# A two-layer hybrid decoder trunk: the mixer's steps in a new order, and sums over feature blocks added by VectorE ahead of one multiplication by ones

## The chip, the cores and the metric

The kernel runs on one NeuronCore of one Trainium2 chip. The metric is the device time of one execution in microseconds (us). The times before the change are 2061.08, 2059.67 and 2060.58 us, median 2060.58. A difference under 0.2%, about 4.1 us, can't be told from none.

## The reference

The input is x (1, 256, 1024), with 256 memory tokens of the same width, all float32. There are two layers (0 and 1), each of three parts with a residual sum behind each:

```
h = h + mixer(rms_norm(h, g_mix))          # 9 column groups of one input projection, three branches, w_out
h = h + cross_attention(rms_norm(h, g_x), rms_norm(mem, g_mem))
h = h + ffn(rms_norm(h, g_f))              # layer 0: dense SwiGLU; layer 1: top 2 of 8 experts
out = rms_norm(h, g_final)
```

The mixer's branches are: A, `silu(layer_norm(conv31(c_a * sigmoid(c_b)))) @ w_conv_out`, where conv31 is a causal depthwise convolution of 31 taps over 512 channels; B, a pooling mixer with a small product `pool_w` and `@ w_pool_out`; C, an mLSTM of 4 heads whose hidden state is normed per head, gated by `sigmoid(z)` and multiplied by `w_mlstm_out`. Each branch is scaled by a sigmoid gate (ga, gb, gc, 1024 columns each), the three are added and multiplied by `w_out`. An RMS norm needs the sum of h² over 1024 features, the layer norm the sum of u and of (u - mean)² over 512.

## The kernel before

**Layout and staging.** Activations lie features first: a tile `[128, 8, 256]` has feature k·128+p in partition p of block k, and 256 tokens. So a sum over features is a sum over partitions and over blocks. TensorE makes it by multiplying with an all-ones matrix, one 256-column product for each block, added in PSUM. All weights pass in chunks of 1 MB (`[128, 2048]` float32): SP loads a chunk into one of 3 `raw` tiles; ScalarE writes its rounded part to one of 3 `w_hi` tiles (`split` on `act`, L685); VectorE writes the rest to `w_lo` (`split` on `dve`, L1079 through `lo`); TensorE makes three products for each block (L1656 to L1658, hi·hi, hi·lo, lo·hi). A chunk of the mixer is 48 products of 256 columns. A `w_hi` tile is free when TensorE has finished the chunk three before it (`pe_chunk`), and SP loads the chunk three on when the VectorE half is done.

**Order.** `MIX` names the mixer's 63 chunks in TensorE's order: cb, ca, q, k, v, pu, z (input columns); gb0, gb1, pw, gb2, gb3; wp0, wp1 (pool output, two PSUM banks each); gc0 to gc3; wm0 to wm3 (mLSTM output); ga0 to ga3; wc0, wc1 (conv output); wo0 to wo3 (w_out); xk0 to xk3, xv0, xq0 to xq3, xv1 to xv3, xo0 to xo3 (attention). Layer 0 then has 33 dense chunks (ff), layer 1 the experts. The programs of ScalarE and VectorE walk the same list by hand: for a step c they do `post(c - 3)`, all work on what chunk c - 3 gave, and then `split(c)`. All engines take their instructions in the order written.

**Places that the change touches.**
- `conv31` deals the taps out to steps by `TAPS`, behind the split; `merge` (wp, wm) multiplies a product in PSUM by its gate and adds it to `xf`. `merge_conv` (wc0, wc1) does that in two halves each and, for each half, waits for ScalarE's rounded part (`merged_hi`, L772) and writes the rest to `a_lo` (`merged_lo`).
- `HIDDEN_T` is the step of gc0. Behind that chunk TensorE turns the normed hidden state (`hidden_transpose`, L1789), for which ScalarE must have scaled it (L840) by reciprocals that VectorE makes (L1310) in step 27. `HIDDEN_STD` is step 26.
- Layer norm: `ln_sums` (L1795) behind wm1 for the sum, behind wm3 for the squares, 4 products each.
- `project_two`: wo0 and wo1 go together. First come blocks 0 to 3 of both, then blocks 4 to 7 of both, so that `a_lo` may be late for the second half.
- `sum_squares` (L1721) is 2 products for each quarter of h. ScalarE squares a quarter into one of two halves of `sq` (in `cacc`). The norm ahead of attention (n = 1) has its quarters behind wo2, wo3, xk0 and xk1; `std` and the norm itself are in ScalarE's and VectorE's step xk1. The norm ahead of the dense part (n = 2, layer 0) has them behind xo1, xo2, xo3 and ff0. Layer 1 has `router_pair` in its place: for each quarter, 4 products for the router's logits (L1731) and 4 for the squares (L1739), tokens in the rows.

Of the kernel before, what the change touches and what calls it, by code (L numbers as in the profile page):

```python
# [22 lines left out]
ALU = mybir.AluOpType  # L23
# [3 lines left out]
P = 128  # L27
# [27 lines left out]
MIX += [("gb", 0), ("gb", 1), ("pw", 0), ("gb", 2), ("gb", 3)] + [("wp", i) for i in range(2)]  # L55
MIX += [("gc", i) for i in range(4)] + [("wm", i) for i in range(4)]
# [128 lines left out]
def trunk(nc, w, out):  # L185
    ctx = ExitStack()
    with ctx:
# [129 lines left out]
        tok_rst, m_scaled = sem("token_rstd"), sem("mem_scaled")  # L317
# [3 lines left out]
        squared = sig("squared", 12)  # L321
        summed = sig("squares_summed", 12)
# [19 lines left out]
        c31_done = sig("conv_done", 1)  # L342
# [334 lines left out]
        def _(act):  # L677
# [116 lines left out]
            def post(layer, j):  # L794

# [17 lines left out]
                elif j in GATE_NO:  # L813
                    gate(layer, j)
                elif kind == "xk":
                    multiplied(layer, j)
                    act.activation(flat(k_t[:, 2 * i:2 * i + 2, :]), bank(("chunk", j))[:, :], ACT.Copy).then_inc(xk_done.sem, 1)

                if j == GATE_ROWS:
                    forget_rows(layer)  # L820
# [41 lines left out]
                if kind == "wc":  # L862
                    for q in (2 * i, 2 * i + 1):
                        merged_hi(layer, q)
# [9 lines left out]
                if XQ0 + 1 <= j < XQ0 + 1 + HEADS:  # L874
                    x_exp(layer, j - XQ0 - 1)
                if XQ0 + 2 <= j < XQ0 + 2 + HEADS:
                    x_copy(layer, j - XQ0 - 2)
                for hd in X_OUT_AFTER.get(j, ()):
                    x_out_hi(layer, hd)
                if XO0 <= j < N_MIX:  # L880
                    if layer and j == XO0:
                        act.activation(warm, eps[:, 0:1], ACT.Sqrt)
                    act.wait_ge(h_att.sem, h_att.at(layer, j - XO0 + 1))
                    if layer == 0:
                        for n in (2 * (j - XO0), 2 * (j - XO0) + 1):
                            ins = act.activation(b_hi[:, n, :], h[:, n, :], ACT.Copy, scale=col(0, R_NORM + 16 + n))
                        ins.then_inc(n_hi.sem, 1)
                    square(layer, 2, j - XO0)
                    if layer:
                        for k in (2 * (j - XO0), 2 * (j - XO0) + 1):  # L890
                            ins = act.activation(xf[:, k, :], h[:, k, :], ACT.Copy, scale=col(0, R_NORM + 16 + k))
                        ins.then_inc(xg_done, 1)
# [35 lines left out]
            def mem_scale():  # L928
                act.wait_ge(tok_rst, 1)
# [8 lines left out]
            def mixer(layer):  # L938
# [6 lines left out]
                if layer:  # L945
                    split(layer, SPL)
                    std(layer, 0)
                    post(layer, 0)
# [92 lines left out]
            for i in range(4):  # L1041

                act.wait_ge(tok_t, 4 + i + 1)
                if i == 0:
                    act.wait_ge(tok_rst, 2)
# [28 lines left out]
        def _(dve):  # L1074
# [63 lines left out]
            def conv31(layer, j):  # L1138

                for pair, k in TAPS.get(j, ()):  # L1140
                    dve.wait_ge(u_done.sem, u_done.at(layer, pair + 1))
                    for c in (2 * pair, 2 * pair + 1):
# [4 lines left out]
                        else:  # L1147
                            ins = dve.tensor_scalar(dst, src, tap, col(0, R_CB + c), ALU.mult, ALU.add)
                        if k == CONV_K - 1 and c == CB - 1:
                            ins.then_inc(c31_done.sem, 1)  # L1150
                        else:
# [1004 lines left out]
```

## Time and profile before

| | before |
|---|---|
| median of three runs | 2060.58 us |
| the profiled execution's own time | 2059.43 us |
| its span, first to last instruction | 2057.7 us |
| TensorE (PE) busy | 2025.9 us, 98% |
| VectorE (DVE) busy | 1631.0 us, 79% |
| ScalarE (ACT) busy | 1304.1 us, 63% |
| mean granted TensorE clock | 0.996 |

In profile lines, PE is TensorE (PEld its weight loads), DVE VectorE, ACT ScalarE and SP the engine that issues the DMAs. A number behind | is busy time, the next the mean of one instruction in ns. Idle time before a group stands with what ended it. A busy PE is counted to the modelled ends of its products, which overlap: the time that a product costs in a stream is the distance of two starts. A float32 product is two records of the profile. In the span, layer 0's mixer and attention last to about 427 us, the dense part to 611, layer 1's mixer and attention to 1036, and the experts to the end.

### The profile page before, as it was taken

The page shows a single profiled execution, that of the slowest core. Times are in us where ns is not written, and L with a number is a line of the kernel's source. Part 1 is how long each engine was busy: PE and PEld are TensorE (multiplying, and loading weights), DVE is VectorE, ACT ScalarE, POOL GpSimd, SP SyncE. Part 2 cuts the span into 40 slices and gives each one's busy share as a digit, 9 for nine tenths or more (in the row PEclk, how much of TensorE's full clock was granted, in tenths as well). Part 3 has the DMA queues.
Part 4 walks back from the last instruction along what each step waited for, and adds up shares of the span by engine and source line. Part 5 has one row for each costly group of instructions (what it writes and reads, how often), then busy time and mean ns, then how long its engine had stood idle before and what let it go on. Part 6 is the DMA issues. An engine that isn't in the chain of part 4 may idle for free.

```text
span 2057.7 us, 33552 instructions
## 1 busy us (share of the span) xinstructions
PE 2025.9 (98%) x12937; PEld 1843.8 (90%) x12937; DVE 1631.0 (79%) x1652; ACT 1304.1 (63%) x1168; POOL 9.3 (0%) x65
## 2 busy tenths in 40 slices
PE   8999999999999999999999999999999999999997
PEld 8999999999999999999988888888888888888886
DVE  6988866555558988866578898888889888898887
ACT  6666454444346566554467777777777777777776
POOL 0000000000000000000000000000000000000000
PEclk9999999999999999999999999999999999999999
DMA  8545545455554545555469999898999989999995
GB/s 251 174 129 165 185 161 187 138 161 189 184 184 142 183 132 164 170 190 164 161 242 375 335 368 372 321 381 325 367 363 345 375 325 370 342 365 375 321 379 188
DMA packets 309916, 527.23 MB, mean 256 GB/s; under 512 B 13598, under 2 KB 156598, under 8 KB 309814
## 3 DMA queue, kind: packets, MB, share of 16 engines
q1 hardware_dynamic: 309814, 525.81, 73.0%
q8 instruction: 72, 1.18, 0.2%
q14 instruction: 30, 0.25, 0.0%
HBM read 524.73 MB, written 1.05 MB: 256 GB/s over the span
## 4 chain that ended last, share of the span: by engine, by line
PE 80%; DVE 9%; ACT 5%; issue 4%; SPq 1%; DMA 0%; DVEq 0%; ACTq 0%
PE ps L1656 25%; PE ps L1658 24%; PE ps L1657 24%; DVE w_lo L1079 3%; ACT w_hi L685 2%; DVE c L1146 1%; PE ps L2027 1%; ACT w_hi L692 1%; PE ps L2102 1%; PE ps L1806 1%; PE ps L1826 1%; DVE a_lo L1079 1%; PE ps L1721 1%; DVE xf L1103 0%; PE ps L1770 0%
## 5 line engine op out<-in xcount | busy, mean ns | idle before, releaser
L1079 DVE TENSOR_TENSOR w_lo<-raw,w_hi 128x2048 fp32r<-128x2048 f32 (+1 forms) x330 | 752.5, 2282 | 246.9 <-ACT w_hi L685 181.9
L1656 PE MATMUL ps<-w_hi,a_hi 128*128 128x512 f32 (+1 forms) x1472 | 566.2, 385 | 2.2 <-DVE w_lo L1079 2.2
L1658 PE MATMUL ps<-w_hi,a_lo 128*128 128x512 f32 (+1 forms) x1472 | 560.5, 381 | 0.0
L1657 PE MATMUL ps<-w_lo,a_hi 128*128 128x512 f32 (+1 forms) x1472 | 559.6, 380 | 0.0
L1656 PE MATMUL ps<-a_hi,w_hi 128*128 128x256 f32 x1456 | 417.4, 287 | 4.0 <-DVE xf L1197 1.9
L1657 PE MATMUL ps<-a_lo,w_hi 128*128 128x256 f32 x1456 | 412.0, 283 | 0.0
L1658 PE MATMUL ps<-a_hi,w_lo 128*128 128x256 f32 x1456 | 411.8, 283 | 0.0
L692 ACT ACTIVATE w_hi<-raw 128x2048 fp32r<-128x2048 f32 x171 | 328.1, 1919 | 122.4 <-PE ps L1658 122.4
L685 ACT ACTIVATE w_hi<-raw 128x2048 fp32r<-128x2048 f32 (+1 forms) x159 | 299.9, 1891 | 59.0 <-PE ps L1658 42.7
L1658 PEld LDWEIGHTS ps<-w_hi,a_lo 128*128 128x128 f32 x1472 | 276.6, 188 | 53.6
L1656 PEld LDWEIGHTS ps<-w_hi,a_hi 128*128 128x128 f32 x1472 | 276.9, 188 | 53.0 <-DVE w_lo L1079 2.8
L1657 PEld LDWEIGHTS ps<-w_lo,a_hi 128*128 128x128 f32 x1472 | 277.0, 188 | 50.7
L1656 PEld LDWEIGHTS ps<-a_hi,w_hi 128*128 128x128 f32 x1456 | 279.2, 192 | 5.7 <-issue 2.2
L1657 PEld LDWEIGHTS ps<-a_lo,w_hi 128*128 128x128 f32 x1456 | 279.3, 192 | 0.5
L1658 PEld LDWEIGHTS ps<-a_hi,w_lo 128*128 128x128 f32 x1456 | 279.1, 192 | 0.0
L1656 PE MATMUL ps<-b_hi,w_hi 128*128 128x256 f32 x808 | 231.5, 286 | 2.5 <-DVE w_lo L1079 1.4
L1657 PE MATMUL ps<-b_lo,w_hi 128*128 128x256 f32 x808 | 228.6, 283 | 0.0
L1658 PE MATMUL ps<-b_hi,w_lo 128*128 128x256 f32 x808 | 228.6, 283 | 0.0
L1656 PEld LDWEIGHTS ps<-b_hi,w_hi 128*128 128x128 f32 x808 | 155.0, 192 | 4.0 <-DVE w_lo L1079 1.8
L1657 PEld LDWEIGHTS ps<-b_lo,w_hi 128*128 128x128 f32 x808 | 155.0, 192 | 0.3
L1658 PEld LDWEIGHTS ps<-b_hi,w_lo 128*128 128x128 f32 x808 | 155.0, 192 | 0.0
L1079 DVE TENSOR_TENSOR w_lo<-mem_t,w_hi 128x2048 fp32r<-128x2048 f32 x56 | 128.4, 2292 | 21.6 <-ACT w_hi L692 21.6
(314 smaller groups left out, 2144.6 us busy)
## 6 DMA issues: line engine op xcount, KB each, us to landing
raw<-in_moe_w SPq DMA_DIRECT2D x171, 1024.0 KB, 6.0
raw<-in_w_in SPq DMA_DIRECT2D x68, 1024.0 KB, 5.2
mem_t<-in_moe_w SPq DMA_DIRECT2D x56, 1024.0 KB, 5.7
area<-in_moe_w SPq DMA_DIRECT2D x56, 1024.0 KB, 5.7
xf<-in_moe_w SPq DMA_DIRECT2D x56, 1024.0 KB, 5.3
raw<-in_ffn_w SPq DMA_DIRECT2D x33, 1024.0 KB, 5.3
raw<-in_w_mlstm_out SPq DMA_DIRECT2D x8, 1024.0 KB, 5.0
raw<-in_w_out SPq DMA_DIRECT2D x8, 1024.0 KB, 5.0
```

The source lines that it names most:

```text
L685: act.activation(w_hi[c % SPL][:, 0:n], raw[c % RAW][:, 0:n], ACT.Copy).then_inc(hi_done.sem, 1)
L692: act.activation(w_hi[m % SPL][:, :], e_raw[m % ERAW][:, 0:CH], ACT.Copy).then_inc(e_hi.sem, 1)
L1079: return dve.tensor_tensor(dst, whole, as_f32(hi), ALU.subtract)
L1146: ins = dve.scalar_tensor_tensor(dst, src, tap, dst, ALU.mult, ALU.add)
L1656: pe.matmul(dst, wh, xh, start=start, stop=False, skip_group_check=True)
L1657: pe.matmul(dst, wh, xl, start=False, stop=False, skip_group_check=True)
L1658: return pe.matmul(dst, wl, xh, start=False, stop=stop, skip_group_check=True)
L1721: ins = pe.matmul(ps[4][:, 0:T], ones[:, :], sq[:, j % 2, i * T:(i + 1) * T], start=(j == 0 and i == 0), stop=(j == 3 and i == 1), skip_gr ...
L1806: ins = pe.matmul(ps[4 + hd % 2][:, tt * T:(tt + 1) * T], q_t[:, k, tt * P:(tt + 1) * P], k_t[:, k, :], start=(tt == 0 and e == 0), stop=( ...
L1826: ins = pe.matmul(ps[X_OUT_BANK[hd]][:, e * T:(e + 1) * T], vx[:, m, hd, e * P:(e + 1) * P], z_sig[:, 4 + 2 * (hd % 2) + m, :], start=(e = ...
L2027: ins = pe.transpose(ps[6][:, k * P:(k + 1) * P], act_e[g % 2][:, k * P:(k + 1) * P], ident[:, :])
L2102: ins = pe.matmul(ps[7 - i][:, k * P:(k + 1) * P], h_tok[:, tt, c:c + P], sel[:, tt, :], start=(k == 0 and tt == 0), stop=(tt == 1), skip_ ...
```

## The change

1. In `MIX`, gc0 moves ahead of wp1. With it `HIDDEN_T` becomes step 28 instead of 29.
2. `post` is cut in two. For a step c, both engines do `first(c - 3)`, `split(c)`, `later(c - 3)`. `first` has what frees PSUM banks, with the merges, `merge_conv` with `merged_hi`, the residual sums and the attention steps. `later` has what remains.
3. `project_two` becomes `project_three`: wo0, wo1 and wo2 go together in the two halves.
4. For three norms (n = 1 of both layers, n = 2 of layer 0) VectorE adds the quarters of squares into one block (`add_squares`), and TensorE makes one product with ones (`sum_added`) instead of eight. It stands behind xk1 for n = 1, and behind ff0 for n = 2. From the third quarter on, ScalarE's square waits for the sum of the quarter before.
5. The layer norm's terms are added by VectorE over blocks (`add_blocks`), one product each instead of four. 
6. In layer 1, three of the router norm's quarters are added by VectorE; the products for squares are 8 at the end instead of 16 spread over the four quarters.
7. One semaphore less: `tok_rst` is replaced by higher counts of `x_scaled`.

```diff
-MIX += [("gb", 0), ("gb", 1), ("pw", 0), ("gb", 2), ("gb", 3)] + [("wp", i) for i in range(2)]
-MIX += [("gc", i) for i in range(4)] + [("wm", i) for i in range(4)]
+MIX += [("gb", 0), ("gb", 1), ("pw", 0), ("gb", 2), ("gb", 3), ("wp", 0), ("gc", 0), ("wp", 1)]
+MIX += [("gc", i) for i in range(1, 4)] + [("wm", i) for i in range(4)]
...
             def square(layer, n, j, src=h):
-                act.wait_ge(summed.sem, summed.at(layer, 4 * n + j - 1))
-                act.activation(sq[:, j % 2, :], flat(src[:, 2 * j:2 * j + 2, :]), ACT.Square).then_inc(squared.sem, 1)
+                if n == 0:
+                    act.wait_ge(summed.sem, summed.at(layer, j - 1))
+                elif j == 0:
+                    act.wait_ge(summed.sem, summed.at(layer, 4 * n))
+                elif j > 1:
+                    act.wait_ge(sq_add.sem, sq_add.at(layer, 3 * (n - 1) + j - 1))
+                act.activation(sq[:, j % 2 if n == 0 else min(j, 1), :], flat(src[:, 2 * j:2 * j + 2, :]), ACT.Square).then_inc(squared.sem, 1)
...
+            def add_squares(layer, n, j):
+
+                dve.wait_ge(squared.sem, squared.at(layer, 4 * n + j + 1))
+                if j > 1:
+                    dve.wait_ge(sq_add.sem, sq_add.at(layer, 3 * (n - 1) + j - 1))
+                ins = dve.tensor_tensor(sq[:, 0, :], sq[:, 0, :], sq[:, 1, :], ALU.add)
+                if j == 3:
+                    ch.link(ins)
+                    ins = dve.tensor_tensor(sq[:, 0, 0:T], sq[:, 0, 0:T], sq[:, 0, T:2 * T], ALU.add)
+                ins.then_inc(sq_add.sem, 1)
+
+            def add_blocks(src, done):
+
+                ch.link(dve.tensor_tensor(cacc[:, 0:2, :], src[:, 0:2, :], src[:, 2:4, :], ALU.add))
+                dve.tensor_tensor(cacc[:, 0, :], cacc[:, 0, :], cacc[:, 1, :], ALU.add).then_inc(done.sem, 1)
...
+                if j == LN_MEAN + 1:
+                    dve.wait_ge(ln_sq.sem, ln_sq.at(layer, 1))
+                    add_blocks(cacc, ln_added)
...
+                if WO0 + 2 <= j < WO0 + 5:
+                    add_squares(layer, 1, j - WO0 - 1)
+                if XO0 + 2 <= j < N_MIX:
+                    add_squares(layer, 2, j - XO0 - 1)
...
                 for c in range(SPL + layer, N_MIX + SPL):
-                    post(layer, c - SPL)
+                    first(layer, c - SPL)
                     if c < N_MIX:
                         split(layer, c, chunk_len(c))
+                    later(layer, c - SPL)
...
-            def project_two(layer, c, xh, xl, ready):
+            def project_three(layer, c, xh, xl, ready):
 
                 for part in range(2):
-                    for j in (c, c + 1):
+                    for j in (c, c + 1, c + 2):
                         if part == 0:
                             pe.wait_ge(lo_done.sem, lo_done.at(layer, j + 1))
                             take_banks(layer, ("chunk", j))
...
+            def sum_added(layer, n):
+                pe.wait_ge(sq_add.sem, sq_add.at(layer, 3 * n))
+                pe.matmul(ps[4][:, 0:T], ones[:, :], sq[:, 0, 0:T], start=True, stop=True).then_inc(summed.sem, 1)
+                pe.sem_inc(summed.sem, 3)
...
+            def router_squares(layer):
+
+                pe.wait_ge(sq_add.sem, sq_add.at(layer, 5))
+                for s in range(2):
+                    if s:
+                        pe.wait_ge(squared.sem, squared.at(layer, 12))
+                    for i in range(2):
+                        for tt in range(TT):
...
+            def ln_sums(layer, done):
+                pe.matmul(ps[5][:, 0:T], ones[:, :], cacc[:, 0, :], start=True, stop=True).then_inc(done.sem, 1)
...
                     if c == LN_MEAN:
-                        pe.wait_ge(c31_done.sem, c31_done.at(layer, 1))
-                        ln_sums(layer, c31, ln_sum)
+                        pe.wait_ge(ln_added.sem, ln_added.at(layer, 1))
+                        ln_sums(layer, ln_sum)
                     if c == LN_VAR:
-                        pe.wait_ge(ln_sq.sem, ln_sq.at(layer, 1))
-                        ln_sums(layer, cacc, ln_var)
+                        pe.wait_ge(ln_added.sem, ln_added.at(layer, 2))
+                        ln_sums(layer, ln_var)
...
-                    if WO0 + 2 <= c < WO0 + 6:
-                        sum_squares(layer, 1, c - WO0 - 2)
+                    if c == WO0 + 5:
+                        sum_added(layer, 1)
...
                     if j == 0:
-                        sum_squares(layer, 2, 3)
+                        sum_added(layer, 2)
```

## Rows read from the trace of the kernel before

**Rows 1.** The page: busy us, share and instructions; granted TensorE clock in 40 slices.

```profile
PE 2025.9 (98%) x12937; PEld 1843.8 (90%) x12937; DVE 1631.0 (79%) x1652; ACT 1304.1 (63%) x1168; POOL 9.3 (0%) x65
...
PEclk9999999999999999999999999999999999999999
```

**Rows 2.** Waits of PE: us in total, how many, longest us.

```profile
PE ps L1656 <- DVE w_lo L1079: 6.3, 9, 1.3
...
PE ps L1656 <- DVE xf L1197: 1.9, 2, 0.9
PE ps L1656 <- DVE a_lo L1079: 1.8, 2, 0.9
...
PE ps L1656 <- issue: 1.1, 2, 0.5
```

**Rows 3.** PE's timeline, layer 0: start us, us, what, [idle before, its releaser].

```profile
192.09 0.28 PE L1658 MATMUL ps<-b_hi,w_lo 128*128 128x256 f32 x1
...
294.17 0.28 PE L1658 MATMUL ps<-a_hi,w_lo 128*128 128x256 f32 x1
295.35 0.39 PE L1656 MATMUL ps<-a_hi,w_hi 128*128 128x256 f32 x1 [0.91 <-DVE a_lo L1079]
...
305.41 0.28 PE L1658 MATMUL ps<-a_hi,w_lo 128*128 128x256 f32 x1
...
306.51 0.28 PE L1657 MATMUL ps<-a_lo,w_hi 128*128 128x256 f32 x1
```

**Rows 4.** PE's groups by line and form: count, busy us, mean ns, idle before.

```profile
L1721 PE MATMUL ps<-cacc,ones 128*128 128x256 f32 x64 | 16.1, 378 | 0.0
...
L1739 PE MATMUL ps<-ones,cacc 128*128 128x1 f32 x32 | 4.1, 250 | 0.0
...
L1795 PE MATMUL ps<-cacc,ones 128*128 128x256 f32 x16 | 3.8, 378 | 0.0
```

**Rows 5.** Two stretches: us, busy PE, PEld, DVE, ACT, POOL, PEclk, DMA, GB/s.

```profile
173.87:198.93 25.06, 24.45 (x196) 23.74 (x194) 22.02 (x39) 12.83 (x16) 0.00 (x0) 1.00 0.55 170
263.95:287.08 23.13, 23.13 (x192) 23.13 (x193) 13.14 (x10) 11.46 (x13) 0.00 (x0) 1.00 0.69 227
```

**Rows 6.** DVE's timeline at wc0 to wo3, layer 0.

```profile
280.71 0.68 DVE L1210 TENSOR_TENSOR area<-area,ps 128x512 f32<-128x512 f32 x1
...
296.41 2.29 DVE L1079 TENSOR_TENSOR w_lo<-raw,w_hi 128x2048 fp32r<-128x2048 f32 x1 [1.11 <-ACT w_hi L685]
...
299.21 3.25 DVE L1348 SCALAR_TENSOR_TENSOR b_lo<-mem_t,par,b_hi 128x256 fp32r<-128x256 f32 x8
```

**Rows 7.** ACT's timeline in the same stretch.

```profile
294.48 1.89 ACT L685 ACTIVATE w_hi<-raw 128x2048 fp32r<-128x2048 f32 x1
296.28 3.30 ACT L867 ACTIVATE b_hi<-mem_t,par 128x256 fp32r<-128x256 f32 x8
299.48 0.62 ACT L696 ACTIVATE cacc<-h 128x512 f32<-128x512 f32 x1
```

**Rows 8.** Timeline of the hidden state's scaling and turning, layer 0, all engines.

```profile
198.93 0.20 DVE L1310 RECIPROCAL small<-small 128x8 f32<-128x8 f32 x1
199.04 1.24 DVE L1197 TENSOR_TENSOR xf<-area,ps 128x512 f32<-128x512 f32 x2
199.16 3.31 ACT L840 ACTIVATE q_t<-q_t,small 128x256 f32<-128x256 f32 x8 [4.06 <-DVE small L1310]
...
205.64 1.91 PE L1789 MATMUL ps<-ident,q_t 128*128 128x128 f32 x16
207.30 0.36 PE L1656 MATMUL ps<-a_hi,w_hi 128*128 128x256 f32 x1
```

**Rows 9.** Layer 1's router: DVE's last residual sum; the chain's piece behind it.

```profile
1032.50 0.69 DVE L1217 TENSOR_TENSOR h<-h,ps 128x512 f32<-128x512 f32 x1 [0.64 <-PE ps L1658]
...
1035.94 3.46 PE ps L1998 x16
```

**Rows 10.** The stretch at L1998, as rows 5: the number behind POOL's is PEclk.

```profile
1035.80:1039.20 3.40, 3.40 (x18) 3.40 (x18) 3.03 (x23) 3.20 (x6) 0.00 (x0) 0.50 0.00 0
```

More of the change, by code:

```diff
@@ L1291, in post, with later @@
                     ins.then_inc(u_done.sem, 1)
+                if j == PW:
+                    multiplied(layer, j)
+                    for g in range(NG):
+                        ins = dve.tensor_scalar(pooled[:, g, :], bank(("chunk", j), g // 2)[:, (g % 2) * HALF:(g % 2 + 1) * HALF], col(0, R_PS + g), None, ALU.mult)
+                    ins.then_inc(pw_done.sem, 1)
+                if kind == "wp":
+                    merge(layer, j, 2 * i, 2)
+                if kind == "wm":
+                    merge(layer, j, 4 + i, 1)
+                if kind == "wc":
+                    merge_conv(layer, j, i)
+                if WO0 <= j < XK0:
+                    residual(layer, j, j - WO0, h_mix)
+                if kind == "xv":
+                    x_value(layer, j, i)
+                if kind == "xq":
+                    multiplied(layer, j)
+                    dve.tensor_copy(flat(q_t[:, 2 * i:2 * i + 2, :]), bank(("chunk", j))[:, :]).then_inc(xq_done.sem, 1)
+                if XQ0 + 1 <= j < XQ0 + 1 + HEADS:
+                    x_probs(layer, j - XQ0 - 1)
+                for hd in X_OUT_AFTER.get(j, ()):
+                    x_out(layer, hd)
+                if XO0 <= j < N_MIX:
+                    residual(layer, j, j - XO0, h_att)
+                    if layer == 0 and j > XO0:
+                        gained_lo(j - XO0 - 1)
+            def later(layer, j):
+                kind, i = MIX[j]
+                if j == GATE_ROWS:
+                    dve.wait_ge(if_mul.sem, if_mul.at(layer, 1))
+                    dve.wait_ge(ifb_in.sem, ifb_in.at(layer, 32))
+                    ch.did(dve.tensor_scalar(rows[:, 0, :], ps[5][0:HEADS, 0:T], if_bias[0:HEADS, :], None, ALU.add))
+                    dve.tensor_scalar(rows[:, 1, :], ps[5][32:32 + HEADS, 0:T], if_bias[32:32 + HEADS, :], None, ALU.add).then_inc(if_dve.sem, 1)
+                if j in QK_NO:
+                    conv4(layer, QK_NO[j])
+                if j == GATE_ROWS + 1:
+                    gate_scans(layer)
+                if j == GATE_ROWS + 6:
+                    dve.wait_ge(if_tr.sem, if_tr.at(layer, 1))
+                    dve.tensor_copy(gcols[:, :], ps[6][:, 0:16]).then_inc(gcols_done.sem, 1)
                 if j == AT["pu", 1]:
@@ L1439, in mixer @@
                     gained_lo(3)
+                    add_squares(layer, 2, 3)
                     ahead(layer, SPL - 1)
@@ L1861, in chunk @@
                     if i == 0:
-                        project_two(layer, c, a_hi, a_lo, y_lo)
-                    elif i > 1:
+                        project_three(layer, c, a_hi, a_lo, y_lo)
+                    elif i > 2:
                         project(layer, c, a_hi, a_lo)
@@ L1896, in mixer @@
                     for j in range(2):
-                        sum_squares(layer, 0, j)
+                        sum_squares(layer, j)
                 for c in range(N_MIX):
@@ L1901, in mixer @@
                         for j in range(2, 4):
-                            sum_squares(layer, 0, j)
+                            sum_squares(layer, j)
                     if layer == 0 and c == 0:
```

153 lines of the change are left out of this document (58 added, 95 removed).

## The prediction

> **What bounds the kernel now.** I read the page first. PE is busy 98% of the span at full clock in nearly all of it [rows 1], so what lengthens or shortens PE's stream moves the end one to one, and an edit on DVE or ACT counts only where PE comes to wait for it. Next the waits of PE: 9 for the low part of weights (6.3 us), 2 for a merge (1.9), 2 for `a_lo` (1.8) and 2 put down to "issue" (1.1) [rows 2]. Then PE's timeline: an idle of 0.91 is 295.35 - 294.17 = 1.18 from start to start, less 0.12 for the product itself, so each wait costs about 0.16 more than its idle [rows 3]. In a stretch without waits 192 products take 23.13 us, 0.12 us each, and a chunk of 48 takes 5.76 [rows 5]. Last, DVE's and ACT's timelines, to see what each wait is behind. All sums below are worked on the profiled execution (own time 2059.43, span 2057.7; the 1.7 around it stay). The median is 1.15 above it, and I add that at the end.
>
> **Products removed.** Two float32 products of `sum_squares` stand between 305.41 and 306.51: 1.10 less two ordinary distances of 0.12 is 0.86, so 0.43 each [rows 3], not the 378 ns times two records that the group shows. The 64 records of L1721 are 32 products [rows 4]. Three norms go from 8 to 1: 21 x 0.43 = 9.0 us. L1795 has 16 records for the squares and as many for the sums, 16 products that become 4: 12 x 0.43 = 5.2. L1739 has 16 products of one column in 32 records [rows 4]; 8 go. Their cost lies between 0.12 (an ordinary one) and 0.43; I take 0.22, since their records of 250 ns are shorter by a third but their starts are set by two weight loads: 1.8 us. Together -16.0.
>
> **Waits removed.** With `split` ahead of the taps, `conv4`, hidden-state work and the norm, all nine waits for low parts should go: 6.3 + 9 x 0.16 = 7.7. That includes the one at xv0, behind the attention norm, 1.3 in each layer. The wait for wp0's merge goes as wp1 now stands between: 2.2. The "issue" waits are at wp1, whose low part came late: gc0 takes its place and is ready: 1.4. The wait for `a_lo` in wo1 goes into another (below): 2.1. Together -13.4. The bounds are 0 and this; they are all in reach, as each is only some 1 us late and at least one piece of DVE work over 1.2 us moves behind its split.
>
> **Wait added 1: the weights of wo2.** `first` holds `merge_conv` and `merged_hi`, so the split of wo2 keeps its place behind wc1's merge. Here DVE and ACT hand each quarter to and fro from 280.71 on; ACT's split of wo2 starts at 294.48 and DVE's ends at 296.41 + 2.29 = 298.70 [rows 6, 7]. wo0 begins at 287.08, the end of the second stretch [rows 5]. In `project_three` the first halves of wo0 and wo1 take 5.76, and at 292.84 PE asks for wo2. It waits 5.86 us, where it now waits 1.06. Nothing ahead shortens this: the chain starts from ga3's end, as PE's two chunks wc0 and wc1 do. Two layers: +11.7. Bounds: 0 if the split came first, which the diff doesn't do, and 11.7.
>
> **Wait added 2: hidden state turned a chunk earlier.** wp0's last product starts at 192.09 [rows 3], so gc0 would end at 192.2 + 5.76 = 197.9. L1310 is now at 198.93, and L840 scales until 202.5 [rows 8]. In `later(27)` the reciprocals have wp0's merge (1.24) and a split (2.29) in front. DVE was idle 25.06 - 22.02 = 3.0 us in the stretch before [rows 5], idle that came from splits waiting for ACT and that the new order fills. So I leave L1310 at 198.9 (bounds 198.9 and 202.4). The last scaling then ends at about 202.3 and its turning, a quarter of the 1.7 us from 205.64 to 207.30 [rows 8], at 202.7; unhindered it would be 199.6. +3.1 a layer, +6.2.
>
> **Wait added 3: one product behind xk1.** Its operand is the last `add_squares`, in step xk0 behind the split of xk3. Counted from W, the end of wo2's split: wo0 ends at W + 5.8, wo1 8.6, wo2 11.5, wo3 17.3, xk0 23.0, xk1 28.8. ACT splits wo3 to 7.7, then rounds the memory (3.30) to 11.0; DVE's part of wo3 ends at 10.0 and of the memory (3.25) at 13.2; then residual sum 0.68, split of xk0 2.29, residual sum, split of xk1: 19.1. From here DVE and ACT alternate: add 0.7 (as L1210), square 0.62, ACT's split 1.9, DVE's 2.29, add, square, copy of xk0 0.6, ACT's split 1.9, DVE's 2.29, and two adds 1.1 (the second half as wide, between 0.35 and 0.7) [rows 6, 7]. With a few hundredths for each hand-over and 0.08 saved where two on one engine overlap, it ends at W + 31.4: wait 2.6, two layers +5.2. Bounds: 0.3 without the backlog (a copy, two splits and two adds take 6.0 against a chunk's 5.76) and 3.0.
>
> **Wait added 4: the squares of the layer norm.** Behind wm1 (at M) the sum comes at M + 0.43, DVE is in wm3's split to about M + 1.7 (my estimate, from its backlog with the last taps). Then come a merge, twice 0.7 (as L1210), a split 2.3 and the centring 1.9 (five instructions of 256 columns, each a little under the 0.41 of L1348's eight): M + 7.2. ACT squares 1024 columns (1.1, between the 0.62 for 512 and the 1.9 for 2048) and splits 1.9, DVE splits 2.3 and adds 1.15: M + 13.5 with the hand-overs [rows 6, 7]. wm3 ends at M + 12.0: 1.5 a layer, +3.0 (bounds 0 and 2). The first sum has 2 us to spare.
>
> **Wait added 5: quarters behind xo.** Without sums between, PE is 0.86 a chunk faster there, while DVE and ACT alternate as in wait 3. In layer 0, `gained_lo(2)` comes 0.7 late for the third pair of blocks in ff0: +0.7. In layer 1 DVE now waits 0.64 for the last xo product [rows 9]; after it, xo3 ends 1.8 earlier (two groups of squares moved back) and DVE comes 2.2 behind it, then residual sum 0.7, logits 0.9 and eight products 1.8, so the turning L1998 starts 5.6 behind xo3, not 3.5: +2.1, of which I've counted none yet. Together +2.9. Later work (`std`, the attention norm 4 us later) has a chunk or more to spare before xq0.
>
> **Sum without the clock.** -16.0 - 13.4 + 11.7 + 6.2 + 5.2 + 3.0 + 2.9 = -0.4 us.
>
> **The clock.** PE now never idles over 1.3 us in the mixers. Where it did little, in the router, the granted clock fell to 0.50 (1.2 GHz) at 1035.80 [rows 10] and is back at 2.4 GHz in the page's slices behind [rows 1]; 16 turnings took 3.46 there against 1.7 at full clock [rows 8, 9], 1.7 us lost. A 5.9 us idle is far more than anything there. I take one such stretch behind each wo2 wait, part of it inside the wait: 1.4 each, +2.8; bounds 0 and 3.4.
> The Trainium skill ("TensorE: Matmul & The Clock Gate", Part 1) says the throttled state is the default and that steady activity releases it. By that rule the long waits cost more than their length, and the trace agrees at the router; no row before shows a long idle inside the mixer.
>
> **Forecast.** -0.4 + 2.8 = +2.4: 2061.8 for the profiled execution, about 2063.0 as median.
>
> **Rivals.**
> 1. The clock holds, only the waits are there: 2060.58 - 0.4 = 2060.2. For it: the mixer's activity on both sides is dense. Against: the router's rows.
> 2. Slower: the clock falls behind the waits of 2 to 3 us also (the turning of the hidden state with single products between pauses, the product behind xk1, two layers): 4 x 1.4 = +5.6 more, 2068.6. It passes +0.2% from the second such fall on.
> 3. Faster: wo2's part is there in time, because `merge_conv` doesn't delay the split as read: +11.7 becomes 0 and so does the clock's 2.8: 2060.58 - 12.1 = 2048.5. If instead waits 2 and 3 don't appear, since DVE is further ahead than the filled idle allows: 2063.0 - 11.4 = 2051.6. Against both: the order in the diff, and a DVE that was 88% busy in the stretch [rows 5].
> 4. The edit does nothing on the path: excluded, as PE is the bound and loses 41 products.
>
> **How the numbers follow.** Chances: forecast with its own range of 2060.6 to 2065.4 (errors of 1 us in the doubled waits) 45%; clock holds 18%; further falls or further waits 22%; a missing large wait 15%. Only the last is faster by over 4.1 us (below 2056.5), with a little from an overvalued pair of small waits: 0.17. Slower (over 2064.7): rival 2, and a fifth of the forecast's own: 0.32. Same: 0.51. The range leaves out a tenth at each end: 2053.0 to 2068.5.
>
> **What would show it.** PE's timeline in both layers: an idle of 5.7 us at wo2, ended by DVE's `w_lo`; idles summing to about 3 in the turning behind gc0; 2 to 3 behind xk1; 1 to 2 behind wm3; no waits at xv0, wp1, ga2 or wm0; PEclk at half for a moment behind wo2. The lines in L1721's place hold 8 + 3 products. I'm wrong if wo2 doesn't wait, or if the sum of idle before PE in the mixers is under 20 or over 40 us.

## The result, and the profile after

| | before | after |
|---|---|---|
| median | 2060.65 us (8 runs, 2059.67 to 2062.26) | 2067.12 us (8 runs, 2063.89 to 2069.06) |
| the profiled execution's own time | 2059.43 | 2067.06 |
| its span | 2057.7 | 2065.2 |
| mean granted TensorE clock | 0.996 | 0.991 |

The ratio is 1.0031, with a 95% interval of 1.002 to 1.0042: slower by 6.5 us, forecast +2.4. The page after, first its busy row (it answers to [rows 1]):

```profile
PE 2017.3 (98%) x12855; PEld 1836.2 (89%) x12855; DVE 1642.0 (80%) x1674; ACT 1304.7 (63%) x1168; POOL 9.2 (0%) x65
```

And the groups of after that stand in the place of L1721, L1739 and L1795 in [rows 4], with their records, two to a product:

```profile
L1759 PE MATMUL ps<-cacc,ones 128*128 128x256 f32 x16 | 3.8, 378 | 0.0
L1788 PE MATMUL ps<-ones,cacc 128*128 128x1 f32 x16 | 3.2, 330 | 0.0
L1844 PE MATMUL ps<-cacc,ones 128*128 128x256 f32 x8 | 2.6, 404 | 2.3 <-DVE cacc L1277 2.3
L1765 PE MATMUL ps<-cacc,ones 128*128 128x256 f32 x6 | 2.0, 413 | 5.4 <-DVE cacc L1271 5.4
```

They are the 41 products fewer. PE is 8.6 us less busy and the span is 7.5 longer, so its idle time grew by 16 us. Part of what is left of the busy time ran at a slower clock, as will be seen. The waits of PE after, beside [rows 2] (us in total, how many, longest):

```profile
PE ps L1694 <- DVE w_lo L1088: 11.5, 2, 5.7
...
PE ps L1765 <- DVE cacc L1271: 5.4, 2, 2.9
PE ps L1839 <- ACT q_t L869: 3.0, 2, 1.5
PE ps L1844 <- DVE cacc L1277: 2.3, 2, 1.2
PE ps L1774 <- DVE h L1226: 1.7, 1, 1.7
```

The nine short waits for weights are two long ones; the merge's `xf`, the `a_lo` of wo1 and the "issue" waits are gone. L1765 is the single product behind xk1, L1839 the turning, L1844 the layer norm's product, L1774 the router's last quarter. PE's timeline of after has each in its place (start, length, what, idle before):

```profile
198.99 3.51 PE L1839 MATMUL ps<-ident,q_t 128*128 128x128 f32 x16 [1.52 <-ACT q_t L869]
...
250.89 0.48 PE L1844 MATMUL ps<-cacc,ones 128*128 128x256 f32 x1 [1.16 <-DVE cacc L1277]
...
297.64 0.58 PE L1694 MATMUL ps<-a_hi,w_hi 128*128 128x256 f32 x1 [5.75 <-DVE w_lo L1088]
298.02 0.41 PE L1695 MATMUL ps<-a_lo,w_hi 128*128 128x256 f32 x1
298.23 0.41 PE L1696 MATMUL ps<-a_hi,w_lo 128*128 128x256 f32 x1
...
331.93 0.48 PE L1765 MATMUL ps<-cacc,ones 128*128 128x256 f32 x1 [2.86 <-DVE cacc L1271]
```

Behind the wait at 297.64 the products start 0.21 apart, not 0.12 as in [rows 3]. DVE and ACT in the same place, beside [rows 6, 7]:

```profile
293.49 0.69 DVE L1088 TENSOR_TENSOR a_lo<-xf,a_hi 128x512 fp32r<-128x512 f32 x1 [0.76 <-ACT a_hi L778]
295.29 2.29 DVE L1088 TENSOR_TENSOR w_lo<-raw,w_hi 128x2048 fp32r<-128x2048 f32 x1 [1.11 <-ACT w_hi L686]
306.07 0.69 DVE L1226 TENSOR_TENSOR h<-h,ps 128x512 f32<-128x512 f32 x1 [8.49 <-PE ps L1696]
```

```profile
293.36 1.89 ACT L686 ACTIVATE w_hi<-raw 128x2048 fp32r<-128x2048 f32 x1
306.13 1.92 ACT L686 ACTIVATE w_hi<-raw 128x2048 fp32r<-128x2048 f32 x1 [10.87 <-PE ps L1696]
```

The split of wo2 does stand behind the merge on both engines and ends at 297.58. Note the two rows behind: DVE then stands idle for 8.5 us and ACT for 10.9, because three chunks give their results together. That comes back at xk1. Stretches of after (us; busy PE, PEld, DVE, ACT, POOL; granted clock; DMA share; GB/s), from wo0's start to the wait, the part of the wait at full clock, the stretch at half clock with the last 1.4 us of the wait in it, and on to wo3's start; then the half clock at the turning of layer 0 and the one behind xk1 of layer 1:

```profile
285.97:291.73 5.76, 5.76 (x50) 5.71 (x48) 4.59 (x5) 0.97 (x2) 0.00 (x0) 1.00 0.33 106
291.73:296.27 4.54, 0.16 (x2) 0.00 (x0) 2.64 (x4) 2.43 (x2) 0.26 (x2) 1.00 0.29 100
296.27:303.10 6.83, 5.46 (x25) 5.46 (x26) 1.31 (x1) 0.00 (x0) 0.00 (x0) 0.50 0.46 154
303.10:311.63 8.53, 8.53 (x74) 8.53 (x72) 4.24 (x6) 5.50 (x10) 0.00 (x0) 1.00 0.00 1
...
200.69:204.10 3.41, 3.41 (x17) 3.27 (x18) 0.00 (x0) 3.38 (x6) 0.00 (x0) 0.50 0.48 166
937.97:941.38 3.41, 3.41 (x19) 3.41 (x18) 3.38 (x3) 0.13 (x1) 0.00 (x0) 0.50 0.69 211
```

In 5.46 us at half clock PE made 5.46 / 0.213 = 25.6 products, which take 3.1 at full clock: 2.4 us lost behind this wait. In layer 1 the half clock begins at 900.42, 2.5 us ahead of the restart at 902.93, so 4.3 of its 6.8 us fall on products and 1.9 are lost. Before the change no stretch at half clock lies between the kernel's first microseconds and the router.

### The profile page after: what moved, and what is told of

It is laid out like the page before. It is cut to its first block, busy times and chain, and to the rows that moved or that the text cites. A ratio compares the mean times of both kernels' runs of the same rounds, so it can differ in the third digit from the quotient of the medians.

```text
span 2065.2 us, 33422 instructions
## 1 busy us (share of the span) xinstructions
PE 2017.3 (98%) x12855; PEld 1836.2 (89%) x12855; DVE 1642.0 (80%) x1674; ACT 1304.7 (63%) x1168; POOL 9.2 (0%) x65
## 4 chain that ended last, share of the span: by engine, by line
PE 83%; DVE 8%; ACT 4%; issue 4%; DMA 0%; DVEq 0%; SPq 0%; POOL 0%; ACTq 0%
PE ps L1694 26%; PE ps L1696 26%; PE ps L1695 25%; DVE w_lo L1088 3%; ACT w_hi L686 2%; PE ps L2076 1%; ACT w_hi L693 1%; DVE c L1155 1%; PE ps L2151 1%; PE ps L1854 1%; PE ps L1874 1%; PE ps L1820 0%; PE ps L2140 0%; DVE h L1226 0%; PE ps L2139 0%
## 5 line engine op out<-in xcount | busy, mean ns | idle before, releaser
L1694 PE MATMUL ps<-a_hi,w_hi 128*128 128x256 f32 x1456 | 418.2, 287 | 13.1 <-DVE w_lo L1088 11.5
```

What stands on the lines that cost most here:

```text
L1694: pe.matmul(dst, wh, xh, start=start, stop=False, skip_group_check=True)
```

## The experiments

Ten kernels ran, each beside the kernel before. The kernel before had a median of 2061.4 beside e1, e2, e4 and e5, 2061.18 beside e6 to e9 and 2060.55 beside e10 and e11; where a kernel is set against the changed one, that is its 2067.12, taken beside a kernel before of 2060.65, so such a difference is uncertain by up to 0.8 us from this alone. None of them leaves out part of the computation; e2 adds some.

### e1: wo2 alone again

```diff
-            def project_three(layer, c, xh, xl, ready):
+            def project_two(layer, c, xh, xl, ready):
...
-                    for j in (c, c + 1, c + 2):
+                    for j in (c, c + 1):
```

> The changed kernel with wo0 and wo1 together and wo2 by itself, as before the change; all else stays changed. Theory (wo2's low part comes late and the long wait also costs clock): both waits of 5.75 us for w_lo go, a wait of about 0.9 for a_lo comes back in each layer (-9.7 us), and the two stretches at half clock behind them go (5.4 us each at half with products running, 2.7 lost each: -5.4). Together -15 against the changed kernel, 2052. Rival A (the wait is of the stage and comes back elsewhere, at wo2 or behind xk1): the idle in wo0 to xk1 stays 8 us a layer and the time within 3 us of the changed kernel's 2067. Rival B (only the wait, clock unchanged): -9.7, 2057.4.

Measured: 2047.44 us (2045.59 to 2048.12), ratio 0.9928 (0.9915 to 0.9942). It is 19.7 less than the changed kernel, more than any term of the prediction. The waits of PE in e1:

```profile
PE ps L1839 <- ACT q_t L869: 3.0, 2, 1.5
PE ps L1844 <- DVE cacc L1277: 2.3, 2, 1.2
PE ps L1694 <- DVE a_lo L1088: 1.8, 2, 0.9
```

The wait of 5.7 is gone and the two for `a_lo` are back, as costed (2 x (5.91 - 1.07) = 9.7). Two further things went that the expectation had not priced: the wait behind xk1 fell from 2.9 and 2.6 to 0.1, and the two short stretches at half clock (at the turning of layer 0 and behind xk1 of layer 1) are gone too; none is left ahead of 1017.0. In the profiled executions, 18.9 us apart, this adds up within 0.5: 9.7 for the waits, 4.3 for the clock behind them (2.4 and 1.9), 5.2 behind xk1 and 2.7 for the two short falls (1.2 and 1.5, see below), less 2.5 for a longer stretch at half clock in the router, 19.4. The fall at the turning lies ahead of wo0, where both kernels are the same, so its 1.2 us are not the group's doing. So the group of three costs three times over: the wait, the clock behind it, and the wait behind xk1, which comes from the backlog on DVE and ACT behind three results that come together.

### e2: PE kept busy during the wait for wo2

44 products of data at hand, into a bank that is not read, stand ahead of wo2's first half. They are extra work in the time in which PE waits.

```diff
+                        if part == 0 and j == c + 2:
+                            for n in range(44):
+                                pe.matmul(ps[6][:, 0:T], wh[:, 0, 0:P], xh[:, 0, :], start=True, stop=True, skip_group_check=True)
```

> The changed kernel with 44 extra products of 256 columns (5.3 us at full clock) into an unused PSUM bank, between the first halves of wo0 and wo1 and the wait for wo2's low part. They add no result. Theory (the idle wait lets the clock fall): the wait for w_lo shrinks to about 0.4 us, wo2 starts at the same place as in the changed kernel, the stretches at half clock behind wo2 go and the time falls by 5.4 us to about 2061.7; the first half of wo2 starts no earlier. Rival (the clock falls for another reason, or its fall costs nothing): the stretches stay, or go with a time within 1.5 us of 2067. Rival (the extra products delay wo2): +1 us or more.

Measured: 2064.94 us (2063.11 to 2066.93), ratio 1.0019 (1.001 to 1.0028), 2.2 less than the changed kernel. The same stretches as of after, in e2, where wo0 starts at 284.68 and wo2 at 296.35:

```profile
291.73:296.27 4.54, 4.15 (x35) 3.95 (x33) 2.96 (x2) 2.24 (x2) 0.09 (x1) 1.00 0.03 11
296.27:303.10 6.83, 6.75 (x56) 6.75 (x57) 0.71 (x2) 0.64 (x1) 0.00 (x0) 1.00 0.45 154
```

The clock stays at 1.00 where it was 0.50, with the weights just as late (wo2 starts 11.67 us behind wo0 in both kernels): the idle is what made it fall. From wo2's restart to the product behind xk1 the time went from 34.29 to 31.91 us in layer 0 and from 33.53 to 31.64 in layer 1: the clock cost 2.4 and 1.9. The profiled executions differ by 3.95 us (2067.06 and 2063.11), near these 4.3. Each has two short falls of 3.4 us at half clock: after at the turning of layer 0 and behind xk1 of layer 1, e2 from 329.18 and from 933.34, behind xk1 of both layers. The medians differ by only 2.2: e2's profiled execution is its fastest, and eight of the other ten had a lower mean clock (0.991 to 0.993 against 0.994). No trace shows where their clock fell. Which of the small falls come is not the same from kernel to kernel.

### e4: the hidden state turned one chunk later

```diff
-HIDDEN_T = AT["gc", 0]
+HIDDEN_T = AT["wp", 1]
```

> The changed kernel with the turning of the hidden state (TensorE) and the gating behind it (VectorE) in the step of wp1 instead of gc0; gc0 stays ahead of wp1. Theory (the turning is one chunk too early for the scaling): the wait for ACT q_t of 1.5 us and the pauses between the heads' products, about 3.1 us together, go in both layers, and with them layer 0's stretch at half clock (1.7 us): -7.9, about 2059.2. Rival (the gating now comes a step later and makes wm0 wait for its hidden state): a wait for b_lo at wm0 of 2 us or more in each layer, and a time within 2 us of 2067.

Measured: 2068.22 us (2066.64 to 2070.62), ratio 1.0031 (1.002 to 1.0042). Nothing gained. Its waits of PE:

```profile
PE ps L1694 <- DVE w_lo L1088: 11.5, 2, 5.7
PE ps L1844 <- DVE cacc L1277: 6.0, 3, 2.9
```

The turning waits no more (in layer 0 gc1 starts 2.45 us earlier than before the change, where in after it starts 1.53 later), but the layer norm's product, 1.2 late in after, is 2.9 late here. PE came earlier and met DVE at the next place where it needs it. In layer 0 the clock fell at that place too (248.52, 6.8 us). In layer 1, where no fall disturbs this piece, wp0 to gc1 is 2.9 us shorter than in after and gc1 to ga1 2.3 longer: 0.6 is left. The price of a wait read at one place is not what its removal gives: that is what is left when the next one has taken its part. The median has a second load: from xo3 to the experts the profiled execution took 26.5 us against 23.9, at half clock for 17.1 us instead of 10.2.

### e5: the attention norm's sums ahead of the split

```diff
                 def first(layer, j):
...
+                if WO0 + 2 <= j < WO0 + 5:
+                    add_squares(layer, 1, j - WO0 - 1)
```

(taken out of `later`; in `first` it stands behind the residual sum)

> The changed kernel with the three add_squares of the attention norm in `first`, ahead of the weights' split, where VectorE now stands idle until ScalarE's part of the split is there. Theory (the product behind xk1 waits for an add that stands behind a split): the waits of 2.9 and 2.6 us behind xk1 shrink to under 0.5 each and layer 1's stretch at half clock behind it goes (1.7): -6.5 to -7, about 2060.3. Rival (the chain of squares and adds is late by itself, after the long wait at wo2, and not for its place): the waits shrink by under 1 us each, the time is within 2 us of 2067.

Measured: 2060.96 us (2057.99 to 2064.46), ratio 1.0 (0.9991 to 1.0009), 6.2 less than the changed kernel. The wait behind xk1 is gone in both layers, and so are both short falls of the clock, of which the one at the turning lies ahead of the edit. The expectation held: the order of a 0.7 us sum and a 2.3 us split on DVE decides 3 us of PE's time.

### e11: wo2's split ahead of the merge, three chunks kept

```diff
+                    if c == WO0 + 2:
+                        split(layer, c, chunk_len(c))
                     first(layer, c - SPL)
-                    if c < N_MIX:
+                    if c < N_MIX and c != WO0 + 2:
```

(on ScalarE and VectorE)

> After with one edit: on ScalarE and VectorE the split of wo2 stands ahead of wc1's merge instead of behind it. The three chunks still go together. Theory (the wait for wo2's weights comes from the merge in front of the split on both engines): PE finds the weights of wo2 in time at about 292.8, does its first half, 2.9 us of work, and then waits for the low part of the merge, which comes 2.3 later than in the kernel before (one split): about 298.7 against 295.7, 3.0 us for each layer in place of 5.9. The clock's fall behind it stays. Median 5.8 less: about 2061. Rival (the merge goes to and fro between the two engines, so a split in front delays each of its steps on both): a wait of 5 or more for a_lo, median 2065 to 2067. In both cases the pair of two (2047) stays ahead.

Measured: 2054.47 us (2053.12 to 2057.75), ratio 0.9974 (0.9965 to 0.9984): 12.7 less than the changed kernel where 5.8 was expected. PE at wo2, and DVE, in e11:

```profile
291.33 0.36 PE L1698 MATMUL ps<-a_hi,w_hi 128*128 128x256 f32 x1 [0.36 <-issue]
```

```profile
285.41 4.50 DVE L1090 TENSOR_TENSOR w_lo<-raw,w_hi 128x2048 fp32r<-128x2048 f32 x2 [1.11 <-ACT w_hi L686]
...
294.76 0.69 DVE L1090 TENSOR_TENSOR a_lo<-xf,a_hi 128x512 fp32r<-128x512 f32 x1 [0.76 <-ACT a_hi L778]
```

The wait is not 3.0 but nothing. The expectation had the low part of the merge at 298.7, which is when wo2's split ended before; it ends at 294.76 + 0.69 = 295.45, 10.4 behind wo0's start at 285.05. The three first halves take 8.6 (and 0.5 at 291.33), and the last two blocks of the second half are needed another 1.4 later, at 10.6. So the merge is in time by 0.2 with three chunks, and with the split behind the merge the weights are 5.9 late. The mechanism named in the prediction, a split of wo2 that stands behind the merge, is shown: e11 takes the wait away by the split's place alone, e1 by asking for wo2 later. What three chunks cost still is the backlog: e11 is 7.0 above e1, and it waits 2.9 and 2.6 behind xk1 as the changed kernel does, with a fall of the clock of 3.4 us at the first of them.

### e8 and e9: the sums alone, the order alone

e8 has e1's pair, the old list and the old order on ScalarE and VectorE, and all sums as changed. The zeroing of three tiles for the experts, which VectorE does behind xo0's residual sum in the changed kernel, is back ahead of it:

```diff
-MIX += [("gb", 0), ("gb", 1), ("pw", 0), ("gb", 2), ("gb", 3), ("wp", 0), ("gc", 0), ("wp", 1)]
+MIX += [("gb", 0), ("gb", 1), ("pw", 0), ("gb", 2), ("gb", 3), ("wp", 0), ("wp", 1), ("gc", 0)]
...
                     first(layer, c - SPL)
+                    later(layer, c - SPL)
                     if c < N_MIX:
                         split(layer, c, chunk_len(c))
-                    later(layer, c - SPL)
```

> One part of the change alone, the sums: the kernel before with all VectorE adds and single products of the change (router's too), but with the old list of chunks, wo0 and wo1 as a pair, and the work of a step ahead of the split again. Theory (products cost PE time one to one; the adds have idle time to lie in when no split stands before them): -16 us for 41 products, +6 for the router's stretch, 2050.6, with the nine waits for w_lo as before. Rival (the adds make PE wait for them or for later splits): waits for cacc or more waits for w_lo of over 3 us in all, and a time over 2055.

e9 has e1's pair, that old list, `split` between `first` and `later` as changed, every sum of squares and terms by products, and the zeroing ahead of the residual sum, as before the change:

```diff
-                if WO0 + 2 <= j < WO0 + 5:
-                    add_squares(layer, 1, j - WO0 - 1)
...
-                    if c == WO0 + 5:
-                        sum_added(layer, 1)
+                    if WO0 + 2 <= c < WO0 + 6:
+                        sum_squares(layer, c - WO0 - 2, 1)
```

> The other part alone, the order: splits between `first` and `later`, old list of chunks, wo0 and wo1 as a pair, all sums by products as before. Theory (weights' low parts come earlier): the nine waits for w_lo (7.7 us) and the late one at wp1 (1.4) go, the wait for the merge (2.2) stays at most, and nothing else changes: 2060.6 - 9.1 = 2051.5. Rival (what stands behind the split becomes late and is waited for instead): new waits of 4 us or more in all and a time over 2056.

Measured: e8 2060.75 us (2058.4 to 2063.27), ratio 0.9997 (0.9988 to 1.0006); e9 2049.13 us (2047.07 to 2049.96), ratio 0.994 (0.9927 to 0.9954). The waits of PE in e8:

```profile
PE ps L1695 <- DVE w_lo L1088: 10.5, 10, 2.0
...
PE ps L1845 <- DVE cacc L1277: 3.4, 2, 1.7
PE ps L1695 <- DVE a_lo L1088: 1.8, 2, 0.9
PE ps L1695 <- DVE xf L1206: 1.8, 2, 0.9
...
PE ps L1775 <- DVE h L1226: 1.7, 1, 1.7
PE ps L1695 <- issue: 1.1, 2, 0.5
PE ps L1766 <- DVE cacc L1271: 1.0, 2, 0.6
```

And the only ones over 0.3 us a piece in the mixers of e9:

```profile
PE ps L1682 <- DVE a_lo L1083: 1.8, 2, 0.9
```

41 products fewer give nothing by themselves in the old order: the weights' waits grow from 6.3 to 10.5 us, and 6.1 us of waits are added at the two new sums and at the router's last quarter. DVE does the sums in time that PE then waits for. The stretch from xo3 to the experts is 4.5 longer than before (24.9 against 20.4), with the router's 1.7 in it. The profiled execution also lost 1.3 us to a fall of the clock at 16.48, which the kernel before doesn't have. The order alone gives 12 us, 11 of them the waits of [rows 2] with their 0.16 each (7.7 + 2.2 + 1.4 = 11.3); even the merge's wait goes without moving gc0. So the move of gc0 bought nothing, and it has a price: from wp0 to gc1 e9 takes 18.95 us in each layer, and e1 21.84. Order, sums and gc0's move together (e1) give 14.0, 2 more than the order. That 2 is what the sums are worth with gc0's move against them; no run has the sums and the new order with the old list.

### e6 and e7: the changed kernel with its waits taken away

e6 joins e1, e4 and e5 and also puts the layer norm's second sum ahead of the split:

```diff
                 def first(layer, j):
...
+                if j == LN_MEAN + 1:
+                    dve.wait_ge(ln_sq.sem, ln_sq.at(layer, 1))
+                    add_blocks(cacc, ln_added)
```

> The changed kernel with all four edits together: wo0 and wo1 in a pair and wo2 alone; the attention norm's adds ahead of the split; the adds of the layer norm's squares ahead of the split too; the turning of the hidden state behind wp1. Against the run with the pair alone (2047.4). Theory (each remaining wait is an add or a scaling behind a split): the waits at the turning (1.5 and pauses, 3.1 us a layer), behind wm3 (1.3, or 3.1 as in the run with the late turning) and behind xk1 (0.3) all go: -9 us, about 2038. Rival (the squares of the layer norm are late since the gating moved a step back, wherever the add stands): the wait behind wm3 stays at 1.5 to 3, 2041 to 2044.

Measured: 2039.53 us (2038.4 to 2041.76), ratio 0.9896 (0.9881 to 0.9911). What is left of waits in the mixers is 1.8 for `a_lo` and under 0.3 a piece elsewhere. e4's edit, worth nothing by itself, is no longer paid for at the layer norm, where the second edit leaves 0.2 of its wait of 2.9. How much each of the four gives in this company wasn't run.

e7 is e6 with the router's part undone: four products for squares behind each quarter, no sums for the router's norm, and the zeroing of three tiles ahead of layer 1's first residual sum behind xo0.

```diff
-                if XO0 + 2 <= j < N_MIX:
+                if layer == 0 and XO0 + 2 <= j < N_MIX:
                     add_squares(layer, 2, j - XO0 - 1)
...
                     router_pair(layer, 3)
-                    router_squares(layer)
```

> The four edits together, and the router's squares as before the change: 16 products spread over the quarters, none added by VectorE, with the zeroing of the three tiles ahead of layer 1's first residual sum as before. Theory (the stretch from xo3 to the experts is longer by 3.5 us in the changed kernel and by 6 with the pair, since the last residual sum comes late, the eight products stand at the end and the clock is at half there): 8 more products cost 1.8 us, that stretch returns to about 20.4 us: -4 us against the four edits. Rival (only the clock's phase makes that stretch long): within 1.5 us of the four edits' time.

Measured: 2037.9 us (2036.9 to 2038.37), ratio 0.9886 (0.987 to 0.9901), 1.6 below e6, where 4 was expected: xo3 to the experts took 23.0 us instead of 26.2, but the products that return cost 1.8 ahead of it. It is the fastest of all, 23.3 below the kernel before (2061.18). Its lead on e6 is small: by the traces 3.2 - 1.8 = 1.4.

### e10: the router's part alone undone

The edit is that of e7, on the changed kernel.

> After with the router's part of the change alone undone: four products for squares behind each of the four quarters, no sums of squares by VectorE for the router's norm, and the zeroing of the three tiles ahead of the residual sum as before. The stretch from the start of xo3 to the experts' first product is 23.9 us in the changed kernel and 20.4 in the one before. Theory (VectorE's two extra sums and the zeroing behind the residual sum stand in the chain to the turning, and ScalarE's last square waits behind a sum): the stretch falls by about 3, the products that return cost about 1.4 ahead of it, median 1.6 to 2.5 less than the changed kernel: about 2065. The expert part's idle of 1.7 before the logits goes. Rival (the stretch is longer since PE now arrives earlier and waits for VectorE's residual sum, whatever is done with the squares): the stretch falls by less than 1, and the median is that of the changed kernel or above it, 2067 to 2069.

Measured: 2064.07 us (2062.7 to 2066.13), ratio 1.0016 (1.0007 to 1.0025), 3.0 less than the changed kernel. PE's timeline of after, behind xo3, and then that of e10; below them DVE's, again of after and then of e10:

```profile
1036.39 0.96 PE L1774 MATMUL ps<-wif,h 128*128 128x8 f32 x8
1039.06 1.06 PE L1774 MATMUL ps<-wif,h 128*128 128x8 f32 x8 [1.71 <-DVE h L1226]
1039.97 3.20 PE L1788 MATMUL ps<-ones,cacc 128*128 128x1 f32 x16
1043.03 3.65 PE L2047 MATMUL ps<-ident,xf 128*128 128x128 f32 x16
```

```profile
1036.81 1.03 PE L1785 MATMUL ps<-ones,cacc 128*128 128x1 f32 x8
1037.71 1.04 PE L1777 MATMUL ps<-wif,h 128*128 128x8 f32 x8
1038.60 1.03 PE L1785 MATMUL ps<-ones,cacc 128*128 128x1 f32 x8
1039.49 3.42 PE L2056 MATMUL ps<-ident,xf 128*128 128x128 f32 x16
```

```profile
1036.11 2.29 DVE L1088 TENSOR_TENSOR w_lo<-raw,w_hi 128x2048 fp32r<-128x2048 f32 x1 [3.37 <-ACT w_hi L693]
1038.32 0.68 DVE L1226 TENSOR_TENSOR h<-h,ps 128x512 f32<-128x512 f32 x1
```

```profile
1033.26 2.29 DVE L1090 TENSOR_TENSOR w_lo<-raw,w_hi 128x2048 fp32r<-128x2048 f32 x1 [3.30 <-ACT w_hi L693]
1036.20 0.69 DVE L1228 TENSOR_TENSOR h<-h,ps 128x512 f32<-128x512 f32 x1 [0.64 <-PE ps L1699]
```

After: the last quarter's logits wait 1.7 for the residual sum, and the eight products for squares follow in one piece, partly at half clock, 0.38 each instead of 0.22. The residual sum is late because a split of weights stands in front of it on DVE, which waited for ACT's part; in e10 that split is 2.85 us earlier, 2.5 when counted from xo3's start. e10: no wait, and the squares lie between the logits. From xo3's start to the experts it takes 20.5 (1030.17 to 1050.67) against 23.9 (1030.56 to 1054.49), as the theory had it. The rival, that an earlier PE has to wait there in any case, falls. The edit also moves the zeroing, but e8, which has the zeroing in its old place and the new squares, waits 1.7 there too: it is the squares. The profiled executions are 3.45 us apart: 3.4 are gained here and 1.8 paid ahead of xo3 for the products. Two falls of the clock of 3.4 us (at the turning of layer 0 and behind xk1 of layer 1), 1.2 and 1.5 us, are absent from this run though the kernel is the same there. About 0.9, lost ahead of the mixer and in the experts, isn't traced.

## Why the prediction was partly right and partly wrong

The time lies in the predicted range, but 4.1 above the number and outside the forecast's own range (2060.6 to 2065.4): what came is nearest to rival 2 (further falls of the clock, 2068.6). That it lies in the range is owed to the range's width; the outcome that was given most weight, no visible difference (0.51), didn't come. Step by step, in the profiled executions, where +2.4 was predicted and +7.6 (span) came:

- **Weights of wo2**: 5.86 a layer predicted, 5.91 from start to start measured (5.75 + 0.16). Right in size and cause, by e1 and e11.
- **Products**: six of L1721's kind between xo0 and ff0 gave 4.78 - 2.40 = 2.38, 0.40 each where 0.43 was taken; the eight one-column products gave 5.88 - 4.09 = 1.79 from xo0 to xo3 of layer 1, 0.22 each as taken. (These are the leads of the kernel before at the starts of the chunks.)
- **Waits removed**: all of those named are gone. Right. By e9 the new order of the splits did this, and for the merge's wait gc0's move wasn't needed. A small wait came that nobody forecast: 0.2 in each layer at pw, for `b_lo`.
- **Turning**: 3.1 a layer predicted, 2.9 measured: 21.84 us from wp0 to gc1 in e1 against 18.95 in e9, which has no such wait. It is made of 1.68 for the first quarter and of three quarters that start 0.80 apart instead of 0.42. Right.
- **Behind xk1**: 2.6 predicted, 3.0 and 2.7 measured, by the backlog that was named; e1 and e5 show both halves of it: no backlog, no wait; the sum ahead of the split, no wait. **Layer norm**: 1.5 predicted, 1.3 measured. **ff0**: 0.7, and 0.75 measured.
- **Router tail**: mis-sized. +2.1 was predicted from xo3 to the experts and 23.93 - 20.42 = +3.5 came. That the turning of the router's stage would be late was right; its start is 6.6 behind xo3's end, not 5.6, as the eight products ran partly at half clock, and 0.4 more was lost behind it. e10 and e8 show that it is the new handling of the squares. The size of the structure's part was right: where old and new handling ran at half clock for the same time, 10.24 us, the stretch is 21.70 (e9) and 23.93 (after), 2.2 apart; for 13.65 us it is 23.0 (e7) and 24.9 (e5 and e8), 1.9 apart. The other 1.3 is more time at half clock, 10.24 us against 6.83 before, a term that the prediction left out here. (Its two terms, 0.7 and 2.1, add to 2.8, where it writes 2.9.)
- **Clock**: the term that was mis-sized most. 1.4 was taken behind each wo2 wait, from a stretch of 3.4 us partly inside the wait; the stretch was 6.8 us long, and e2 shows a cost of 2.4 and 1.9, +1.5 in all. Two more falls came that were rival 2's: at the turning of layer 0, where wp0 to gc1 takes 23.05 us against 21.84 in layer 1 with the same waits (+1.2), and behind xk1 of layer 1, where xk2 to xq0 takes 18.95 against 17.45 in layer 0 (+1.5).

The errors add up: clock 1.5 + 1.2 + 1.5, router 1.4, xk1 0.5, turning -0.4, layer norm -0.4, together 5.3 where 5.2 are missing. Smaller ones of both signs, as at pw, are left out, so that the sum closes this well is in part chance. Nearly all of what is missing is clock: 4.2 in the mixers and 1.3 in the router.

The prediction's own sign of being wrong, an idle of PE in the mixers under 20 or over 40 us, didn't show: the waits of after give 11.5 + 5.4 + 3.0 + 2.3, the pauses in the turning 0.7 and pw 0.4, 23.3 in all. Of the rivals, that the clock holds (2060.2) is refuted by the rows at half clock, and that a large wait is missing by the waits of after. The Trainium skill ("TensorE: Matmul & The Clock Gate", Part 1), as the prediction cited it, has steady activity release the clock: e2 agrees, with 1.00 in place of 0.50.

**Left open**: what decides whether the clock falls at a wait of 1.7 to 3 us. After has a fall at the turning of layer 0 and not of layer 1, e10 at neither, with the same instructions. Behind xk1, with waits of 2.9 and 2.6 us in each of them, after has a fall in layer 1, e2 and e4 in both layers, e11 in layer 0 and e10 in neither. And in the router the time at half clock differs from kernel to kernel with the same instructions there. The stretches from xo3 to the experts, of after and of e11:

```profile
1030.56:1054.49 23.93, 20.93 (x141) 20.78 (x140) 12.57 (x49) 11.32 (x17) 0.00 (x0) 0.79 0.41 146
```

```profile
1014.36:1040.63 26.27, 23.27 (x140) 23.12 (x140) 12.58 (x49) 11.32 (x17) 0.00 (x0) 0.68 0.42 151
```

DVE and ACT do the same work in the same busy time; PE is granted 0.79 or 0.68, and the stretch is 2.3 longer. So 2 us of any comparison here hang on where the clock's fall begins; it takes nothing from the differences of 6 us and more on which the main points rest. Those of e2, e7 and e10, 1.6 to 3 us, rest on the stretches of their traces and not on their medians.

## What to carry to other kernels

Work moved off the bound engine gives nothing where it lands ahead of what that engine waits for next: 41 products less gave 0, the order of splits and slack work alone 12, and both, with two of the sums put ahead of the next split, the turning a chunk later and the pair in place of the three, 22. When several chunks are grouped to hide one late operand, ask where the weights of the last one stand in the other engines' queues, and what those engines do while no result comes: here the group of three saved a wait of 1 us, made one of 6, idled VectorE for 8.5 us and passed the backlog on to the next sum. Price each long wait of TensorE with the slow clock behind it, here 1.9 to 2.4 us on 5.8.

## What the runs showed of the hardware

- Around an idle of 5.75 us amid dense products the granted clock was 0.50 (1.2 GHz) for 6.8 us in both layers, with products 0.21 apart instead of 0.12. It fell 1.4 us before PE restarted in layer 0 and 2.5 us before in layer 1, and so cost 2.4 and 1.9 us. In e4's layer 1 the same idle brought only 3.4 us at 0.50. With products in place of the idle it stayed at 2.4 GHz (e2).
- It fell also where PE had waited only 1.5 us and then turned small tiles with pauses (200.69, 3.4 us at half), and 1.5 us behind the end of a wait of 2.6 (937.97, 3.4 us), but not in each layer nor in each kernel.
- In the router, where PE makes products of 1, 8 and 128 columns, the clock stayed at half for 3.4 to 17.07 us in one piece, by kernel; with the same instructions there, for 6.8 (after) to 17.07 (e1, e11).
